# Two blocks on one Trainium2 core: first weight tile taken in among the transposes, filter rows loaded early, pool products earlier on VectorE, and two stages merged into one

## The reference

```python
# first block
h = rmsnorm(x, pre_norm_g); q, k, v, g_a, u_p, g_p = split(h @ w_in)     # 1024 -> 2304
a = banded_attention(q, k, v, rel_bias[bucket(key - query)], sink) * silu(g_a)   # 8 heads, |rel| <= 128
p = multiscale_pool(u_p, pool_w, pool_scale) * silu(g_p)                 # windows 2, 4, 8, 16
x = x + rmsnorm(concat(a, p) @ w_out, post_norm_g)
# second block
proj = rms_norm(x, pre_norm_w) @ w_in_2                                  # 1024 -> 7168
x0, x1, v = split(short_conv(hy_in)); k = hyena_filter(L, ...)           # 3 small sine layers of position
y_a = x0 * long_conv(v * x1, k) * silu(hy_gate)                          # length 4096 transform
y_b = sg_u * (sgu_w @ head_norm(sg_v) + sgu_b) * silu(sg_gate)           # per chunk of 128 tokens
out = x + rms_norm(concat(y_a, y_b) @ w_out_2, post_norm_w)
```

## Time and profile before

| | us |
|---|---|
| median of three executions | 3296.18 (3294.19 to 3310.67) |
| profiled execution, its own time | 3311.16 |
| span of the profiled execution | 3309.3 |
| TensorE, VectorE, ScalarE, GpSimd busy | 3039.7, 2556.7, 803.2, 325.2 |

### The profile page before, as it was taken

One profiled execution on the slowest core, in us unless ns is written; L12 is line 12 of the kernel. 1 busy time (PEld: TensorE's weight loads), 2 busy tenths in 40 slices (PEclk: granted clock), 3 DMA queues, 4 the chain that ended last, 5 costly groups with the idle time before them and its releaser, 6 DMA issues. The chain is left out here.

```text
span 3309.3 us, 32983 instructions
## 1 busy us (share of the span) xinstructions
PE 3039.7 (92%) x12882; PEld 2190.8 (66%) x12882; DVE 2556.7 (77%) x2800; ACT 803.2 (24%) x1362; POOL 325.2 (10%) x468
## 2 busy tenths in 40 slices
PE   6999999888885998999999999999888989889999
PEld 4444444656674777777788888887655656577887
DVE  6979999598895795999999999994368879762221
ACT  2000000486232321000011111111244625531110
POOL 3212120000111450000000000000000000000000
PEclk8999999999997998999999999999999999969999
DMA  6555552201346444656645544531131321334321
GB/s 204 144 174 150 137 151 57 109 1 53 117 143 217 153 134 115 181 158 159 177 137 140 145 128 129 146 95 45 46 130 48 136 108 51 140 130 131 102 90 51
DMA packets 209467, 402.28 MB, mean 122 GB/s; under 512 B 20944, under 2 KB 132368, under 8 KB 201440
## 3 DMA queue, kind: packets, MB, share of 16 engines
q1 hardware_dynamic: 185568, 316.78, 31.5%
q0 software_dynamic: 22592, 75.01, 8.6%
q10 hardware_dynamic: 1152, 8.39, 0.7%
HBM read 322.50 MB, written 81.81 MB: 122 GB/s over the span
## 5 line engine op out<-in xcount | busy, mean ns | idle before, releaser
L1665 PE MATMUL PS<-HH,WH 128*128 128x512 f32 x1536 | 611.0, 398 | 37.3 <-DVE WL L1562 18.3
L1667 PE MATMUL PS<-HH,WL 128*128 128x512 f32 x1536 | 610.3, 397 | 0.0
L1666 PE MATMUL PS<-HL,WH 128*128 128x512 f32 x1536 | 610.2, 397 | 0.0
L782 PE MATMUL PS<-M 128*128 128x512 f32 x1152 | 501.5, 598 | 15.1 <-DVE M L605 12.6
L782 PEld LDWEIGHTS PS<-M 128*128 128x128 f32 x1152 | 220.2, 192 | 295.8 <-issue 279.2
L1665 PEld LDWEIGHTS PS<-HH,WH 128*128 128x128 f32 x1536 | 291.5, 190 | 108.6 <-DVE WL L1562 18.7
L1666 PEld LDWEIGHTS PS<-HL,WH 128*128 128x128 f32 x1536 | 291.8, 190 | 67.0
L1667 PEld LDWEIGHTS PS<-HH,WL 128*128 128x128 f32 x1536 | 291.8, 190 | 65.7
L109 DVE SCALAR_TENSOR_TENSOR HP<-MF,HP 128x1024 f32<-128x1024 f32 x252 | 323.4, 1283 | 8.0
L2399 PE MATMUL PS<-WH,YH 128*128 128x512 f32 x512 | 201.2, 393 | 14.3 <-DVE WL L2370 9.1
L109 DVE SCALAR_TENSOR_TENSOR M<-M 128x1024 f32<-128x1024 f32 x160 | 205.6, 1285 | 7.1 <-DMA M<-c_feat 1.5
(11 more groups left out here) (222 smaller groups left out, 5082.5 us busy)
## 6 DMA issues: line engine op xcount, KB each, us to landing
MF<-h_scratch SPq DMA_DIRECT2D x380, 256.0 KB, 4.3
M<-c_feat POOLq DMA_DIRECT2D x194, 256.0 KB, 4.3
MF<-w_in SPq DMA_DIRECT2D x56, 512.0 KB, 4.5
M<-u_scratch SPq DMA_DIRECT2D x16, 1024.0 KB, 4.7
M<-c_decay POOLq DMA_DIRECT2D x48, 256.0 KB, 2.9
M<-w_in SPq DMA_DIRECT2D x18, 512.0 KB, 5.1
M<-x SPq DMA_DIRECT2D x16, 512.0 KB, 4.1
x_scratch<-M SPq DMA_DIRECT2D x16, 512.0 KB, 5.0
```

The lines of the kernel that those rows point to most:

```text
L782: ins = t.matmul(PS[:, banks + c, :], wt[:, k], HT[:, k, TC * c:TC * c + TC], start=(k == 0), stop=(k == KD - 1))
L1665: t.matmul(dst, wh, hh, start=(k == 0), stop=False)
L1666: t.matmul(dst, wh, hl, start=False, stop=False)
L1667: ins = t.matmul(dst, wl, hh, start=False, stop=(k == KD - 1))
```

## The change

- The first weight tile is loaded with x (after its fifth chunk), and its 32 products (four column groups of 512 tokens by eight k) are cut: two behind the transposes of each block from 5 on, the other ten behind the last. x comes in nine chunks. Odd blocks are scaled on ScalarE, behind the next block's square.
- The first four filter rows are loaded by SyncE behind x; GpSimd loads from the fifth on.
- The bias table is no longer turned with FLIP on TensorE: SyncE stores it 128 times over (2 MB) before weight tile 8, and loads BIAS_MADE from it, with a step that turns it, before tile 10.
- `filter_rows` is 3 before L605 and 3 after.
- At the end of attention FH 1 and WOH 1 stand behind the last step; in the output product FH for block i+2 stands before the square of X1, and three of the sine operations before FL.
- The two program blocks of `second_inputs` are one. The values use banks 2 to 7, their bias products 0 and 1; WH and WL of the first two tiles are made during the last step, each as soon as the quarter of WVH or WVL under it has been used. SV_OPS has 20 operations fewer; the rule behind x0 6 takes them up.

```diff
     def row(r):
-        v.wait_ge(row_in[r % 4], 32 * (r // 4 + 1))
+        if first_rows_in is None:
+            v.wait_ge(row_in[r % 4], 32 * (r // 4 + 1))
+        elif r < 4:
+            v.wait_ge(first_rows_in[r], 32)
+        else:
+            v.wait_ge(row_in[r % 4], 32 * (r // 4))
         return rows[r % 4]
...
-X_CHUNKS = (0, 2, 4, 8, NT)
+X_CHUNKS = (0, 1) + tuple(range(2, NT + 1, 2))
...
+    wv = A["w_in"][0].rearrange("(k p) e -> p k e", p=P)
     for c in range(1, len(x_in)):
         tokens(c)
+        if c == 4:
+            sp.dma_start(WB[:, 0], wv[:, :, tiles1[0][2]:tiles1[0][2] + P]).then_inc(w_in_sem[0], 16)
+    for r in range(4):
+        filter_row(sp, ROWS[r], A["c_feat"], FILT, r, first_rows_in[r])
     sp.dma_start(PSC, A["pool_scale"]).then_inc(const_in, 16)
...
-    wv = A["w_in"][0].rearrange("(k p) e -> p k e", p=P)
     for j, (kind, g, e0) in enumerate(tiles1):
+        if j == 0:
+            continue
+        if j == 8:
+            sp.wait_ge(rel_out, 1)
+            sp.dma_start(rel_d[:, :, 0:REL], RELO[0:H, :].unsqueeze(1).to_broadcast([H, P, REL])).then_inc(rel_stored, 16)
+        if j == 10:
+            sp.wait_ge(rel_stored, 16)
+            sp.dma_start(BIAS_MADE, bass.AP(rel_d.tensor, P - 1, [[REL, P], [P * (REL + 1), H], [1, W_KEYS]])).then_inc(bias_in, 16)
...
-    g.wait_ge(rel_out, 1)
-    g.dma_start(rel_d, RELO[0:H, :]).then_inc(rel_stored, 16)
     for i in range(NT):
         g.wait_ge(ssq_done, i + 1)
         rsqrt(RS[:, i:i + 1], SSQ[:, i:i + 1], D, rstd_done)
-        if i == 2:
-            g.wait_ge(rel_stored, 16)
-            g.dma_start(HK, bass.AP(rel_d.tensor, 0, [[1, P], [REL, H], [1, W_KEYS]])).then_inc(hk_in, 16)
-    g.wait_ge(ht_done, NT)
-    g.wait_ge(flip_mm, 2)
-    for r in range(ROWS_OF(FILT)):
-        if r >= 4:
-            g.wait_ge(row_used, r - 3)
+    for r in range(4, ROWS_OF(FILT)):
+        g.wait_ge(row_used, r - 3)
         filter_row(g, ROWS[r % 4], A["c_feat"], FILT, r, row_in[r % 4])
...
+    def scale_odd(i):
+        s.wait_ge(rstd_done, i + 1)
+        s.activation(X[:, i], X[:, i], ACT.Copy, scale=RS[:, i:i + 1]).then_inc(x_scaled[1], 1)
+
     for i in range(NT):
...
         s.activation(JUNK, X[:, i], ACT.Square, accum_out=SSQ[:, i:i + 1]).then_inc(ssq_done, 1)
+        if i and i % 2 == 0:
+            scale_odd(i - 1)
+    scale_odd(NT - 1)
...
             s.wait_ge(scores_done, len(STEPS))
-            for i in range(2):
-                features_high(i)
-                weights_high(i)
+            features_high(0)
+            weights_high(0)
+    weights_high(1)
+    features_high(1)
     for k in range(2, KD):
         weights_high(k)
...
+        if i + 2 < NT:
+            features_high(i + 2)
         s.wait_ge(x1_done, i + 1)
...
-        if i + 2 < NT:
-            features_high(i + 2)
         s.wait_ge(x1rstd_done, i + 1)
...
     for i in range(NT):
-        if i in (11, 13):
-            half = (i - 11) // 2
-            v.wait_ge(flip_mm, half + 1)
-            v.tensor_copy(BIAS_MADE[:, 4 * half:4 * half + 4], PS[:, 0:4, 0:W_KEYS]).then_inc(bias_done, 1)
-        v.wait_ge(rstd_done, i + 1)
-        v.tensor_scalar(X[:, i], X[:, i], RS[:, i:i + 1], None, ALU.mult).then_inc(x_scaled, 1)
+        if i % 2 == 0:
+            v.wait_ge(rstd_done, i + 1)
+            v.tensor_scalar(X[:, i], X[:, i], RS[:, i:i + 1], None, ALU.mult).then_inc(x_scaled[0], 1)
...
         ins.then_inc(pool_y, 1)
-        filter_rows(5)
+        filter_rows(3)
...
                                op1=ALU.mult).then_inc(pt_done, 1)
-        filter_rows(1)
+        filter_rows(3)
...
-    for i in range(2):
-        features_low(i)
-        weights_low(i)
+    features_low(0)
+    weights_low(0)
     gate(len(STEPS) - 1)
+    weights_low(1)
+    features_low(1)
     for k in range(2, KD):
...
         if i:
             features_out(i - 1)
+        first_layer_work(3)
         if i + 2 < NT:
             features_low(i + 2)
-        first_layer_work(7 if i < 7 else 6)
+        first_layer_work(4 if i < 7 else 3)
         if i == NT - 1:
             first_layer_work(total - pos[0])
...
     def transposes(i, src, scaled, evac, done):
-        t.wait_ge(scaled, i + 1)
+        if scaled is x_scaled:
+            t.wait_ge(scaled[i % 2], i // 2 + 1)
+        else:
+            t.wait_ge(scaled, i + 1)
...
+    first_pieces = [(c, k) for c in range(NTC) for k in range(KD)]
+
+    def first_tile(n):
+        for _ in range(n):
+            c, k = first_pieces.pop(0)
+            ins = t.matmul(PS[:, c, :], WB[:, 0, k], HT[:, k, TC * c:TC * c + TC], start=(k == 0), stop=(k == KD - 1))
+        return ins
+
     for i in range(NT):
         transposes(i, X[:, i], x_scaled, ht_done, x_transposed)
-        if i in (8, 11):
-            half = (i - 8) // 3
-            t.wait_ge(hk_in, 16)
+        if i == 5:
             t.wait_ge(rel_out, 1)
-            if half:
-                t.wait_ge(bias_done, 1)
-            for r in range(4):
-                ins = t.matmul(PS[:, r, 0:W_KEYS], FLIP, HK[:, 4 * half + r], start=True, stop=True)
-            ins.then_inc(flip_mm, 1)
+            t.wait_ge(w_in_sem[0], 16)
+        if i >= 5:
+            first_tile(2)
     t.wait_ge(ht_done, NT)
-    t.wait_ge(bias_done, 2)
+    first_tile(len(first_pieces)).then_inc(proj_done, 1)
     t.wait_ge(const_in, 16 * NCONST)
-    loads = [0, 0, 0]
+    loads = [16, 0, 0]
     for j, (kind, g, _) in enumerate(turns1):
+        if j == 0:
+            continue
         banks = 4 * (j % 2)
...
-    @block.scalar
-    def _(s_):
+    def values_scalar(s_, ahead_of_last):
...
+            if s == STEPS - 1:
+                ahead_of_last()
...
-                s_.activation(CN[s % 2][:, P * a:P * a + P], PS[:, s % 6, P * a:P * a + P], ACT.Identity,
+                s_.activation(CN[s % 2][:, P * a:P * a + P], PS[:, 2 + s % 6, P * a:P * a + P], ACT.Identity,
...
-    @block.vector
-    def _(v):
+    def values_vector(v, ahead_of_last):
...
+            if s == STEPS - 1:
+                ahead_of_last()
             v.wait_ge(sv_done, s + 1)
             for a in range(4):
-                v.bn_stats(ST[:, a], PS[:, s % 6, P * a:P * a + P]).then_inc(stats_done, 1)
...
-            if s == NT - 1:
+            if s in (NT - 1, STEPS - 1):
                 ins.then_inc(quarter_done, 1)
...
     @block.sync
     def _(sp):
+        values_sync(sp)
+
...
         raw_next(0)
         raw_next(1)
+        for b in range(2):
+            sp.wait_ge(vn_stored[b], 16 * NT)
         for d in range(2):
             sp.dma_start(CC[HID * d:HID * d + HID, 0:CH], A["filt_w_out_2"][:, D * d:D * d + CH]).then_inc(kept.first_in, 16)
...
     @block.gpsimd
     def _(g):
+        values_gpsimd(g)
+        for b in range(2):
+            g.wait_ge(vn_stored[b], 16 * NT)
+        g.wait_ge(sv_done, STEPS)
         vnr = vn_d.rearrange("(i p) (h d) -> h p i d", p=P, d=P)
...
-        weights_high(0)
-        weights_high(1)
+        def first_high():
+            for w in range(2):
+                s.wait_ge(quarter_done, 5 + w)
+                weights_high(w)
+
+        values_scalar(s, first_high)
...
-        weights_low(0)
-        weights_low(1)
+        def first_low():
+            for w in range(2):
+                v.wait_ge(quarter_done, 7 + w)
+                weights_low(w)
+
+        values_vector(v, first_low)
...
     @block.tensor
     def _(t):
+        values_tensor(t)
+
...
                 t.wait_ge(wl_done, NV + w + 1)
                 for c in range(NTC):
+                    if j == 0:
+                        t.wait_ge(bias_done, 2)
+                        if c >= 2:
+                            t.wait_ge(vn_done, 4 * (STEPS - 3 + c))
                     dst = PS[:, banks + c, :]
...
-SV_OPS = [0] * 8 + [3] * 24
+SV_OPS = [0] * 8 + [3] * 8 + [2] * 12 + [1] * 4
```

More of the change, by code:

```diff
@@ L91, in halve, with filter_op @@
     link(v.tensor_tensor(low, x, high, ALU.subtract))
-def filter_op(v, link, W, q, acc, bufs, rows, row_in, row_used):
+def filter_op(v, link, W, q, acc, bufs, rows, row_in, row_used, first_rows_in=None):
     total, back, miss = bufs
@@ L223, in first_block @@
         pool_step = sem("pool_step")
-        x_scaled = sem("x_scaled")
+        x_scaled = [sem("x_scaled%d" % i) for i in range(2)]
         x_transposed = sem("x_transposed")
@@ L237, in first_block @@
         row_in = [sem("row1_in%d" % i) for i in range(4)]
+        first_rows_in = [sem("first_row_in%d" % i) for i in range(4)]
         row_used = sem("row1_used")
@@ L318, in _ @@
             tokens(0)
-            for dst, name in ((RELT[0:32, :], "c_bucket"), (RELM[0:H, :], "c_relmask"), (RELB[0:32, :], "rel_bias"),
-                              (FLIP, "c_flip")):
+            for dst, name in ((RELT[0:32, :], "c_bucket"), (RELM[0:H, :], "c_relmask"), (RELB[0:32, :], "rel_bias")):
                 sp.dma_start(dst, A[name]).then_inc(rel_in, 16)
@@ L615, in _ @@
```

(53 more changed lines are left out.)

22 lines of the change are left out of this document (8 added, 14 removed).

## The result

The changed kernel takes 3251.1 us (median of 6, 3240.4 to 3255.7), the kernel before in the same comparison 3296.9 (3294.2 to 3313.0). The ratio is 0.984, 95% interval 0.981 to 0.987. It is faster, as forecast, but by 46 us and not by 75. 0.984 of the 3296.2 shown at first is 3244, at the upper end of the range; the median itself is 6 us above it.

What follows compares the result with a forecast made beforehand. TensorE or VectorE was taken to lead, stage by stage. Gains of 23.5, 12.6, 4, 1.5, 15.5 and 18.5 less 0.5 made 75.1 us; 3296.2 less that is 3221.1, given as 3222, range 3206 to 3245.

Steps and rivals of the forecast that it cites:

- Part 1: Opening: first weight tile's products among the transposes, TensorE leading from block 5 at 2.95 us a block; gain 23.5 us.
- rival B: Opening stays at the low clock, turn 0 ending at about 73: 3233 us; chance 0.13.
- Part 2: First projection: fewer filter operations ahead of L605 remove three TensorE gaps, gain 12.6 us, and slow products behind them, 4.
- Part 3: First projection: the bias table's 2 MB store and 1.5 MB load on SyncE's queue cost or gain nothing.
- Rival F: First projection: the table's 2 MB store from 8 partitions blocks SyncE's queue, slower than before, 3712 us at worst; chance 0.01.
- Part 4: End of attention: ScalarE does only FH 0 and WOH 0 ahead of the last turned copies; gain 1.5 us.
- Part 5: Output product: FH before the square of X1 closes VectorE's 1.12 us hole per block; gain 15.5 of 16.9 us.
- rival C: Output product: GpSimd's rsqrt is held up until VectorE reads PSUM again, so no gain there: 3237 us; chance 0.09.
- Part 6: Boundary before the second projection: TensorE waits about 2.5 us, not 18.3, and should keep the high clock; gain 18.5 us.
- Rival E: Boundary stays because the WR, WH and WL hand-over waits for stores as before: 3237 us; chance 0.04.
- Part 7: Second projection: the 20 moved filter operations return, WL for v 6 just in time; loss 0.5 us, up to 4.
- Rival D: Second projection: the 20 operations aren't covered, a lag of 10 to 20 at v 6 costs TensorE as much: 3237 us; chance 0.08.

Runs made afterwards that it cites:

- e6: Changed kernel with all 32 products of the first weight tile behind the last transpose, none among the transposes: 3256.1 us, ratio 0.985.
- e8: Changed kernel with the copy of w_out before tile 17, the bias table's store before tile 18 and its load behind the loop: 3238.9 us, ratio 0.979.
- e5: Changed kernel with FH again behind the square of X1 in the output product, three sine operations kept before FL: 3248.8 us, ratio 0.982.
- e9: Changed kernel with the filter's second angle behind hgate 6 instead of x0 6 in the second projection: 3241.2 us, ratio 0.980.
- e7: Changed kernel with filter_rows again 5 before L615 and 1 behind it: 3278.6 us, ratio 0.991.
- e3: Changed kernel with SV_OPS as before the change, 24 steps of 3 filter operations: 3244.2 us, ratio 0.979.
- e2: Changed kernel with the bias table's store before weight tile 14, its load before 16 and the copy of w_out before 13: 3244.2 us, ratio 0.981.

## Why the forecast was right in sign and 29 us too large

**Part 1, the opening: right, and too careful.** 29.2 against 23.5. The block costs 2.59 and not 2.95, and the slow start that was priced at 2.5 did not come: rival B is rejected by a clock of 1.00 from 18 us on. Forecasting TensorE as the leader from block 5 was right; e6 shows what leads without the products.

**Part 2, pool products: the order right, the size not.** The step that failed first is "only three gaps, 12.6 us together, are VectorE's fault", put down to 50 operations at 1.26. The 16.82 us that VectorE waited for PT, in the same timeline, had no place in it. Against the second execution of before, 515.6 us, the projection of the changed kernel is 6.9 us longer, not shorter.

**Part 3, the table: this is the step that failed.** "Nothing, below or above" was argued from one load of as many runs beside x. That argument asked whether SyncE's own queue and the weight tiles would suffer. What suffered was GpSimd's queue, whose 256 KB rows VectorE needs every few us. A row's load issued at 144.04, 1.2 us behind the copy of w_out, landed at 163.81, and one issued at 193.08, behind the table's store, at 218.16; the median is 4.3 us. Together the transfers cost 11.4 us of the projection: 522.5 with them there, 511.0 with them behind the last pool group (e8), which is the forecast stage to the us. 8.4 of it are TensorE's two gaps, and most of the rest slow products behind the second (granted clock 0.72 from 408 to 420). The copy of w_out, which both kernels have, shares that: e8 moved it too. What the table's transfers alone cost was not tried. Rival F did not come; its reading of the 16 KB store was off as well, since 1.53 in the earlier trace rows is idle time that ended with the store's landing, at 15.88, 5.7 us after its issue.

**Part 4:** 1.0 against 1.5.

**Part 5: the gain right, the cause half wrong.** 16.4 against 15.5, and 18.6 when undone. But the part was named for FH ahead of the square, and e5 shows that this added nothing; the three operations ahead of FL were enough. GpSimd's two operations take 1.05 and 1.53 beside VectorE's run, as the earlier trace rows had them, and VectorE has no hole between X1 starts 12.35 apart: rival C is rejected. The rule named with it (the Trainium skill, "SBUF — State Buffer", Who interferes with whom) gives the ports to whichever of the two instructions starts first, for that instruction; taken as a block over VectorE's whole run it does not agree with the trace, where GpSimd has both done at 953.4, inside the run from 946.91 on.

**Part 6, the boundary:** wait 2.13 against 2.5. The forecast 18.5 are 15.8 of waiting and 2.7 of slow products in the first tile, and the table has only the waiting, 16.2; the first tile stands in the table's row below. There the evacuation starts 23.9 us after the first product, against 25.1 before, so that the part gave 17.4 in this execution. "Should keep the high clock" failed here and held in six of the eleven profiles: 22.3, which makes the part 19. Rival E is rejected.

**Part 7, the 20 operations:** "the cover is used to the last half us" was right in kind and off in size: a wait of 5.93 and, by e9, 7.7 us with the clock's fall, against 0.5. That WL would be what v 6 waits for was named as a sign of error. Rival D had the mechanism, at half its price. The gain of 1.3 in the table comes from the first profile of before, where the products stood 0.232 us apart in the last two thirds of the stage. In its second profile they stand 0.229 apart, as in the changed kernel, and the stage takes 1119.5: against that the changed kernel is 7.2 us longer, as the loss at v 6 has it. What sets the pace was not found.

**What no part had:** 9.6 us in the long convolution and 3.1 in the values. Both come and go between executions of one kernel: 572.0 and 195.8 us in the second profile of before. The forecast took the 15 us between the profiled execution of before and the median to be outside its sum, and they were partly inside it: the 12.6 of gaps and 8.5 us of the second projection were of that execution. What the rest of the spread between executions is made of was not settled.

The table's differences from the forecast add up: +5.7 opening, -11.3 projection, -0.5, +0.9, -3.1 values, -2.3 boundary, +1.8, -9.6 convolution, +0.5 make -17.9, which is 75.1 less 57.2. The medians differ by 45.8, another 11 less: the profiled execution of before, 3311.2, is as slow as the two slowest of its six (3310.7, 3313.0), and that of the changed kernel is above its median by less. Against the second profile of before the differences come to 50.3: 27.5 gained in the opening, 2.5 in attention, 17.9 in the output product, 16.1 at the boundary and 1.5 in the second output product, and 6.9, 7.2 and 1.1 lost in the two projections and the convolution.

## What to carry to other kernels

A large transfer that nothing waits for has a price on the queues that it does not stand in: look for the small loads of the other engines in its time, and put it where those have slack. Before pricing a gap, read all waits of the engine blamed for it, a transfer's landing too, and look at a second execution if there is one. Where a hole is an engine waiting for another, independent work moved into it can close it by itself; an earlier result on top of that added nothing here.

## What the runs showed of the hardware

- **Two transfers issued together.** A 1 MB store issued 0.01 us behind a 4 MB copy between DRAM tensors held its reader up by 16.82 us in one execution and by 2.58 in another. Loads of 256 KB on another queue, with a median of 4.3 us to landing, took about 20 us behind the 4 MB copy and up to 25.1 behind the 2 MB store (changed), and VectorE waited up to 12.63 us for one (e7).
- **The clock after a short wait.** After 2.13 us without a product, at the same place in eleven profiles, the granted clock fell to the lower level, 1.2 GHz, for 3.4 us in five and stayed at 1.00 in six; the first tile takes 1.5 us longer where it fell. After 18.29 us, after 9.69 (e3) and after 5.93 at v 6 (nine profiles) it fell each time. Behind the 5.93 it cost 1.5 us in the changed kernel and 2.4 in e2 (third angle against e9, from the start of v 6). What decides after the short wait is open.
- **The low clock in the long convolution.** Its code is the same in all kernels, and its length roughly follows the time that the granted clock is low in it: 71 us low in the profile of before and in e6, length 563.6 and 562.6; 87 in e2 and e3, 568.2 and 569.5; 92 in changed, 573.2; 93 in before again, 572.0; 99 in e5, 576.4. What chooses it is open. The windows of the stage, before and changed:

```profile
2380.00:2944.00 564.00, 478.08 (x2213) 326.48 (x2212) 438.20 (x560) 275.30 (x467) 25.98 (x49) 0.94 0.28 99
```

```profile
2314.00:2887.00 573.00, 486.34 (x2212) 330.23 (x2210) 438.46 (x560) 275.00 (x467) 25.91 (x49) 0.92 0.27 97
```

- **Two paces at full clock.** Products of the same shape stand 0.233 us apart in the values, in every profile, and 0.229 in the second projection of changed (nine steps in 2.10, ten in 2.29 in its timeline below). In the first profile of before the second projection has 0.232 in its last two thirds, so the stage does not settle it:

```profile
1182.46 0.39 PE L1398 MATMUL PS<-WVL,HH 128*128 128x512 f32 x1
...
1184.56 0.40 PE L1398 MATMUL PS<-WVL,HH 128*128 128x512 f32 x1
...
1194.05 0.39 PE L1701 MATMUL PS<-HH,WL 128*128 128x512 f32 x1
...
1196.34 0.39 PE L1699 MATMUL PS<-HH,WH 128*128 128x512 f32 x1
```

Over the 4,608 products of the second projection the difference of the two would be 20 us, by estimate. Why there are two was not found.
